# Address steps of 16 bytes more between FFN operand tiles and between the slots of the split weights

## The reference

```
for i in range(2):
    a = rmsnorm(h, norm_mix[i])
    h = h + (mla(a), swa_sinks(a))[i]            # 16 heads / 32 query heads, 4 kv heads
    u = rmsnorm(h, norm_ffn[i]) @ w_in[i]        # [256, 2048] x [2048, 2*5632]
    c = conv_b + u[t-2]*conv_w[0] + u[t-1]*conv_w[1] + u[t]*conv_w[2]
    gate, val = split(c, 2)
    h = h + (silu(gate) * val) @ w_out[i]        # [256, 5632] x [5632, 2048]
return rmsnorm(h, final_norm)
```

## Time and profile before

| | |
|---|---|
| median of 3 runs | 1994.18 us (1993.44 to 1996.38) |
| profiled execution, its span | 1992.6 us |
| instructions | 33224 |
| TensorE busy, matmuls | 1979.7 us, 99% |
| VectorE busy | 1418.9 us, 71% |
| ScalarE busy | 992.0 us, 50% |
| granted TensorE clock, mean | 0.999 |

### The profile page before, as it was taken

One profiled execution on the slowest core, in us unless ns is written; L12 is line 12 of the kernel. 1 busy time (PEld: TensorE's weight loads), 2 busy tenths in 40 slices (PEclk: granted clock), 3 DMA queues, 4 the chain that ended last, 5 costly groups with the idle time before them and its releaser, 6 DMA issues.

```text
span 1992.6 us, 33224 instructions
## 1 busy us (share of the span) xinstructions
PE 1979.7 (99%) x11726; PEld 1746.3 (88%) x11726; DVE 1418.9 (71%) x1969; ACT 992.0 (50%) x1180; POOL 143.9 (7%) x157
## 2 busy tenths in 40 slices
PE   9999999999999999999999999999999999999998
PEld 8998888888888888888899899888888888888886
DVE  6856788877887786554567668788778877865444
ACT  6556445555545554343455654554555555534433
POOL 1112220000000000110120004100000000011000
PEclk9999999999999999999999999999999999999999
DMA  8566655555555555556575445655555556676654
GB/s 299 177 196 161 196 188 189 177 200 191 189 175 193 193 194 192 190 176 205 191 237 179 132 136 179 197 184 178 190 193 195 189 183 196 207 235 213 200 188 137
DMA packets 106870, 379.67 MB, mean 191 GB/s; under 512 B 12107, under 2 KB 12684, under 8 KB 106668
## 3 DMA queue, kind: packets, MB, share of 16 engines
q1 hardware_dynamic: 102332, 362.22, 54.7%
q0 software_dynamic: 4176, 16.07, 3.2%
q10 hardware_dynamic: 288, 0.33, 0.1%
HBM read 368.09 MB, written 10.49 MB: 190 GB/s over the span
## 4 chain that ended last, share of the span: by engine, by line
PE 96%; DVE 2%; DMA 1%; SPq 0%; ACT 0%; issue 0%; ACTq 0%
PE ps L429 46%; PE ps L432 24%; PE ps L823 4%; PE ps L822 4%; PE ps L821 4%; PE ps L723 2%; PE ps L725 2%; PE ps L724 2%; DMA raw<-weights 1%; DVE w_lo L1172 1%; PE ps L761 1%; PE ps L784 1%; PE ps L459 1%; PE ps L460 1%; PE ps L458 1%; PE ps L772 1%
## 5 line engine op out<-in xcount | busy, mean ns | idle before, releaser
L1172 DVE TENSOR_TENSOR w_lo<-raw,w_hi 128x1024 fp32r<-128x1024 f32 (+1 forms) x678 | 824.9, 1230 | 498.5 <-ACT w_hi L861 477.2
L861 ACT ACTIVATE w_hi<-raw 128x1024 fp32r<-128x1024 f32 (+1 forms) x678 | 710.4, 1054 | 778.4 <-PE ps L432 454.9
L429 PE MATMUL ps<-op_in,w_hi 128*128 128x512 f32 x2992 | 1026.4, 391 | 1.7 <-DVE w_lo L1205 0.9
L432 PE MATMUL ps<-op_in,w_lo 128*128 128x256 f32 x2992 | 812.3, 282 | 0.0
L429 PEld LDWEIGHTS ps<-op_in,w_hi 128*128 128x128 f32 x2992 | 548.9, 188 | 106.1 <-issue 1.3
L432 PEld LDWEIGHTS ps<-op_in,w_lo 128*128 128x128 f32 x2992 | 564.8, 189 | 15.7
L429 PE MATMUL ps<-op_ffn,w_hi 128*128 128x512 f32 x704 | 243.1, 390 | 0.0
L432 PE MATMUL ps<-op_ffn,w_lo 128*128 128x256 f32 x704 | 195.8, 282 | 0.0
L429 PEld LDWEIGHTS ps<-op_ffn,w_hi 128*128 128x128 f32 x704 | 131.1, 188 | 26.5
L821 PE MATMUL ps<-w_hi,op_ffn 128*128 128x512 f32 x352 | 139.5, 396 | 0.0
L822 PE MATMUL ps<-w_lo,op_ffn 128*128 128x512 f32 x352 | 139.5, 396 | 0.0
(11 more groups left out here) (218 smaller groups left out, 2052.4 us busy)
## 6 DMA issues: line engine op xcount, KB each, us to landing
raw<-weights SPq DMA_DIRECT2D x662, 512.0 KB, 4.1
raw<-weights SPq DMA_DIRECT2D x16, 384.0 KB, 3.1
bias_rows<-brow POOLq DMA_DIRECT2D x1, 6144.0 KB, 36.1
win_bias<-bias_rows POOLq DMA_DIRECT2D x4, 1024.0 KB, 8.4
h<-xt SPq DMA_DIRECT2D x8, 256.0 KB, 7.2
raw<-weights SPq DMA_DIRECT2D x8, 256.0 KB, 6.2
x_tok<-x_rows SPq DMA_DIRECT2D x4, 512.0 KB, 8.7
h_rows<-h_blocks POOLq DMA_DIRECT2D x16, 128.0 KB, 5.5
```

The costliest lines, as they stand in the source:

```text
L429: return mm(ps[:, bank, 0:2 * T], whi, op, start=start, stop=stop)
L432: return mm(ps[:, bank, 0:T], wlo, op[:, 0, :], start=False, stop=False)
L861: f(w_hi[s][:, 0:cols], raw[s][:, 0:cols], ACT.Copy).then_inc(hi_ready, 1)
L1172: v.tensor_tensor(w_lo[s][:, 0:cols], raw[s][:, 0:cols], w_hi[s][:, 0:cols].bitcast(F32), ALU.subtract).then_inc(lo_ready, 1)
```

## The change

The two rings of split weights become one tensor each, in which a slot takes 1028 floats instead of 1024; each slot is still used for 1024. The tiles of both FFN operands take 516 floats instead of 512, and the second operand lies 32 bytes behind the first instead of 64. The parameter tile is cut to the 832 columns that are loaded, from 896. Offsets modulo 128 afterwards: w_hi slots 0, 16, 32, 48; w_lo slots 64, 80, 96, 112; op_in, op_att, op_lat 32; tile k of op_ffn[0] 32 + 16k, of op_ffn[1] 64 + 16k. The list of instructions of each engine, their shapes and their waits are the same in both kernels.

```diff
+SLOT_STEP = CH + 4
+TILE_STEP = 2 * T + 4
...
-    w_hi = [new(f"w_hi{s}", [P, CH], F32R) for s in range(SLOTS)]
-    w_lo = [new(f"w_lo{s}", [P, CH], F32R) for s in range(SLOTS)]
+    ring_hi, ring_lo = new("ring_hi", [P, SLOTS, SLOT_STEP], F32R), new("ring_lo", [P, SLOTS, SLOT_STEP], F32R)
+    w_hi = [ring_hi[:, s, 0:CH] for s in range(SLOTS)]
+    w_lo = [ring_lo[:, s, 0:CH] for s in range(SLOTS)]
...
-    par = new("par", [P, 7 * P])
+    par = new("par", [P, PC_END])
...
-    rg = region(FT * 2 * T * 4 + 64)
+    rg = region(FT * TILE_STEP * 4 + 32)
     r_o = rg + 57344
-    op_ffn = [place("op_ffn0", [P, FT, 2, T], F32R, rg), place("op_ffn1", [P, FT, 2, T], F32R, rg + 64)]
+    op_ffn = [place(f"op_ffn{k}", [P, FT, TILE_STEP], F32R, rg + 32 * k)[:, :, 0:2 * T].rearrange("p k (s t) -> p k s t", s=2)
+              for k in range(2)]
```

## The result

| | before | after |
|---|---|---|
| median us | 1994.18 (3 runs) | 2005.25 (2004.94 to 2005.26, 3 runs) |
| span of the profiled execution | 1992.6 | 2003.4 |

The kernel is slower: the ratio is 1.0053, with a 95% interval of 1.0039 to 1.0067. That is 11 us, and the profile has 10.8 of them.

A forecast was written before the change was run, and what follows sets the result against it. The prediction took TensorE's queue of matmuls, busy 99% with almost no waits, as the bound. Its terms, all 0, gave 1992.6 + 0 = 1992.6 us in a profiled span, 1994.2 in a run; range 1982 to 2010.

The forecast's parts named there:

- likeliest case: Whole kernel: low address bits have no effect, 1994.2 us in a run, own range 1992 to 1997; chance 0.42.
- (a): TensorE's matmuls: a step does not depend on low address bits, 0 us, with bounds of -150 and +24 us.
- two hints: TensorE: steps exceed their columns with nothing waited for; 512 columns cost 5 to 6 ns more in f1_out than in pairs.
- slower rival: The 4144 pairs: slot offsets leave a good relation, 5.8 ns a pair, +6.0 to +18.0 us, middle 2004; chance 0.31.
- faster rival: Matmuls: low address bits clash today and the stagger thins it out, 1988, 1957 or 1844 us; chance 0.27.
- (b): ScalarE and VectorE write the split operands at new places: cost 0 unless a split takes 60% longer.
- (c): Parameter tile shortened to the loaded columns, op_ffn 16 bytes more a tile, same transfers: cost 0.

The follow-up runs named there:

- second sweep: Kernel before with op_in at 80 (112 in f1_in), op_ffn[0] at 96, op_ffn[1] at 32 modulo 128, slots unmoved: 2014.26 us.
- third sweep: Kernel before with op_ffn[0] 4 bytes on, op_in for f1_in 8 bytes on, op_ffn[1] at 16 modulo 128: 1999.24 us.

## Why the prediction was right or wrong

*The forecast was the wrong case.* Its likeliest case, no effect of the low address bits, did not happen; the case that did was the second, slower, at 0.31, whose middle (2004) lies 1 us from the result. The range held.

*The step that failed is (a), whose value was put at 0.* Measured, it is +11.1 us over the phases. I took the 0 from rows that compared different blocks, slots and tiles and found the step constant. But all of them lie whole multiples of 512 bytes apart, and the effect has a period of 256. The rows could not show it. The text said so, that bits 4 to 8 had not varied, and then gave these rows the deciding weight. The two hints it put aside were the real ones: a step longer than its columns with nothing waited for, and f1_out's 234.3 ns. At (0, 0) this came down to 226.7. The bound of (a) that put the whole excess on addresses was not reached: the best placement left 340 ns a pair against 320 for its columns, and 226.7 against 213.3.

*The slower rival held in kind; its size was partly luck.* It named the slot offsets, chunks that differ by slot, and 5.8 ns a pair in one to three slots of four. Measured: in slots 0 and 1 (2827 - 2773) / 8 = 6.7 ns a pair, in slots 2 and 3 0.5. The 5.8 came from f1_out, where the roles of the operands are exchanged, and no run ties it to the pairs; nothing shows that its nearness to 6.7 is more than chance. Nor does the loss need the stagger: w_lo's 64 bytes, which the rival listed among the offsets and did not price by themselves, are enough. With no stagger at all, at (160, 96), f0_in takes 497.3 us, more than the 493.4 of the changed kernel. Its guess that slot 2 would be bad, where w_hi and the operand start alike, was wrong: modulo 256 they are 128 apart, and that slot is one of the good ones.

*The faster rival held in one phase.* f1_out gained 2.5 us. The objection to it, that stagger only helps where today's relation is worse than the mean, fits the direction of every phase. The mean of the staggered phases is near 232 ns for 512 columns (f0_out 232.2, f1_out 231.6 to 232.1 by line, f0_in 233.2); f1_out was above it at 234.3, the feature kind below at 228.5 to 229.0. (In the feature kind the 256 columns beside them gave back 0.6 to 1.2 ns, 117.1 to 117.7 against 118.3.)

*The skill's rule on ports.* By the Trainium skill, "SBUF — State Buffer", section "Who interferes with whom", TensorE's two read ports are independent and it never waits on anyone; the prediction took from this that offsets between the operands mean nothing. Here the measurement differs: w_lo moved by 64 bytes with w_hi and op_att in place, and a_out's chunk went from 2773 to 2827 ns. That the two reads get in each other's way is the plainest account of a relation with a period, but it is argued, not shown: no run took the loads away, and it does not say why one pair can have two times.

*(b) and (c) held*: VectorE's split 1231 ns against 1230, ScalarE's 1054 in both, and TensorE's waits fell.

## What to carry to other kernels

Where TensorE waits for nothing and a matmul still takes longer than its columns, the places of its two operands are worth a run: this kernel lost 0.5% or gained 1.3% by them alone. Look for one good fixed relation and keep every tile and slot on it, by steps that are multiples of the period; a stagger gave about the mean here. Check every group of chunks and not one stretch alone, since some relations have two times; (64, 0) and (32, 32) had one. A trace tests an address bit only if that bit varies in it.

## What the hardware showed that I had not expected

- Where the moving and the stationary operands start relative to each other, modulo 256 bytes, changes the step of fp32r matmuls: a pair of 512 and 256 columns takes 340 to 354 ns (2720 to 2835 ns a chunk), 512 columns in f1_out 226.7 to 234.4, always at the full granted clock.
- The best relation of those tried depends on the kind of matmul: (0, 0) is best in f1_out and poor in pairs, (64, 0) best in pairs and poor in f1_out (2813 ns a chunk). The kinds differ in order, columns and roles, and which of these counts is open.
- One relation can have two times. At (224, 224) the first group of f0_out took 2773 ns a chunk and the others 2827 (second sweep); at (160, 32) it was 2773 and 2800, at (0, 192) 2773 and 2827. What picks the time is open.
- Constant pairs give times in a few steps, 2720, 2747, 2773, 2800 and 2827 ns a chunk for many, 27 ns apart; others, such as 2784, 2789 and 2811 in f1_out, lie between.
- A moving operand 4 bytes off, at (164, 164), took 54 ns a chunk more than (160, 160) in another phase; 8 bytes off, at (40, 40), took no more than (32, 32) (f0_out and f1_in of the third sweep).
